# Recurrence of the gated linear attention: forward logarithm and scan moved ahead of the backward gates, sigmoid's table loaded by a one-element activation

## The reference, cut to what matters

```
u = h @ w_in                          # 2048 x 10240
q, a_f, a_b, i, z = split(u, 5)
log_f = logaddexp(log(lb), log1p(-lb) + log_sigmoid(a))   # = log(lb + (1 - lb) * sigmoid(a))
key   = (1 - lb) * sigmoid(-a)
# forward and backward, per head: b = cumsum(log_f); scores = q k exp(b_t - b_s), t >= s; out = scores @ v
o = rms_norm(o_fwd + o_bwd, o_norm)
return (o * silu(z)) @ w_out
```

## Time and profile before

| | |
|---|---|
| Median of 3 runs | 1899.51 us (1898.82 to 1900.25) |
| Profiled execution, first to last instruction (span) | 1896.9 us |
| Runs' median less the span | 2.6 us |
| TensorE busy | 1891.0 us (100%) |
| VectorE, ScalarE, GpSimd busy | 1288.3, 1058.0, 624.8 us |
| Granted TensorE clock | full speed in all 40 slices |
| DMA | 352.64 MB, mean 186 GB/s |

### The profile page before, as it was taken

The page is one execution under the profiler, slowest core; times in us unless marked ns, Lnnn a source line. Parts: engine busy times, 40 slices in busy tenths (PEclk is TensorE's granted clock), DMA queues, the critical chain, the costliest instruction groups (busy, mean ns, idle before and its releaser), DMA issues.

```text
span 1896.9 us, 28820 instructions
## 1 busy us (share of the span) xinstructions
PE 1891.0 (100%) x10856; PEld 1558.4 (82%) x10856; DVE 1288.3 (68%) x1871; ACT 1058.0 (56%) x1402; POOL 624.8 (33%) x657
## 2 busy tenths in 40 slices
PE   9999999999999999999999999999999999999999
PEld 8888878888887888788888888888888888888887
DVE  5899967555888888887668876555555555544443
ACT  7444466456868787875465755444444444443432
POOL 1899852306051423302408643222222222210000
PEclk9999999999999999999999999999999999999999
DMA  9666656666555565555565555666666666666564
GB/s 326 193 190 186 178 170 196 189 194 183 168 175 166 151 187 166 169 158 187 189 189 147 155 177 176 201 193 195 188 192 196 194 192 193 194 193 195 192 196 157
DMA packets 183600, 352.64 MB, mean 186 GB/s; under 512 B 11840, under 2 KB 12352, under 8 KB 183488
## 3 DMA queue, kind: packets, MB, share of 16 engines
q1 hardware_dynamic: 183344, 351.12, 61.1%
q10 hardware_dynamic: 144, 0.01, 0.0%
HBM read 348.99 MB, written 2.10 MB: 185 GB/s over the span
## 4 chain that ended last, share of the span: by engine, by line
PE 88%; DVE 4%; POOL 4%; issue 2%; ACT 2%; DVEq 1%; POOLq 0%; ACTq 0%
PE acc L625 28%; PE acc L627 28%; PE acc L626 28%; POOL kb L503 2%; POOL kf L503 1%; DVE w_lo L1271 1%; PE T L576 1%; DVEq L1257 1%; PE acc L592 1%; PE T L740 1%; PE T L841 0%; ACT w_hi L887 0%; PE T L731 0%; DVE Xc L1459 0%; PE T L820 0%
## 5 line engine op out<-in xcount | busy, mean ns | idle before, releaser
L1271 DVE TENSOR_TENSOR w_lo<-raw,w_hi 128x1024 fp32r<-128x1024 f32 x564 | 695.2, 1235 | 516.5 <-ACT w_hi L887 507.3
L887 ACT ACTIVATE w_hi<-raw 128x1024 fp32r<-128x1024 f32 x655 | 687.5, 1057 | 609.8 <-PE acc L627 587.4
L625 PE MATMUL acc<-w_hi,h_hi 128*128 128x512 f32 x1872 | 735.5, 393 | 1.1 <-DVE w_lo L1271 1.0
L627 PE MATMUL acc<-w_hi,h_lo 128*128 128x512 f32 x1872 | 728.8, 389 | 0.0
L626 PE MATMUL acc<-w_lo,h_hi 128*128 128x512 f32 x1872 | 728.7, 389 | 0.0
L625 PEld LDWEIGHTS acc<-w_hi,h_hi 128*128 128x128 f32 x1872 | 351.4, 188 | 80.4 <-issue 4.5
L627 PEld LDWEIGHTS acc<-w_hi,h_lo 128*128 128x128 f32 x1872 | 351.4, 188 | 73.7
L626 PEld LDWEIGHTS acc<-w_lo,h_hi 128*128 128x128 f32 x1872 | 351.5, 188 | 71.1
L565 POOL COPY fT<-fq 32x256 f32<-32x256 f32 x176 | 110.9, 630 | 387.4 <-DVE fq L1753 380.5
L474 POOL TENSOR_TENSOR w_lo<-raw,w_hi 128x1024 fp32r<-128x1024 f32 x80 | 190.5, 2411 | 68.0 <-ACT w_hi L887 67.8
L1362 DVE SCALAR_TENSOR_TENSOR T<-vpad,feat,T 128x256 f32<-128x256 f32 x464 | 182.5, 482 | 0.0
(11 more groups left out here) (256 smaller groups left out, 1564.8 us busy)
## 6 DMA issues: line engine op xcount, KB each, us to landing
raw<-in_hgrn_w_in_dram SPq DMA_DIRECT2D x160, 512.0 KB, 3.7
raw<-in_conv_w_in_dram SPq DMA_DIRECT2D x96, 512.0 KB, 4.2
raw<-in_ffn_w_gate_dram SPq DMA_DIRECT2D x88, 512.0 KB, 4.4
raw<-in_ffn_w_up_dram SPq DMA_DIRECT2D x88, 512.0 KB, 4.3
raw<-in_ffn_w_down_dram SPq DMA_DIRECT2D x88, 512.0 KB, 4.2
raw<-in_attn_w_qkv_dram SPq DMA_DIRECT2D x40, 512.0 KB, 3.7
raw<-in_conv_w_out_dram SPq DMA_DIRECT2D x32, 512.0 KB, 4.4
raw<-in_hgrn_w_out_dram SPq DMA_DIRECT2D x32, 512.0 KB, 4.5
```

The costliest lines, as they stand in the source:

```text
L625: nc.tensor.matmul(o, hi[:, kt, a], w_hi[:, slot, kk, :], start=c == 0 and kk == 0, stop=False)
L627: last = nc.tensor.matmul(o, lo[:, kt, a], w_hi[:, slot, kk, :], start=False, stop=c == p.chunks - 1 and kk == CK - 1)
L887: A(w_hi[:, slot, :, :], raw[:, slot, :, :], ACT.Copy).then_inc(hi_ready, 1)
L1271: TT(w_lo[:, slot, :, :], raw[:, slot, :, :], rounded(w_hi[:, slot, :, :]), ALU.subtract).then_inc(split_ready, 1)
```

## The change: what it does

- `ln_f(j, 0)` moves from hook 6 to hook 3 (behind `raw_out`), and waits for `gates(j, 0)` alone; `ln_f(j, 1)` stays at hook 7. The order of `g_act` is now gates 0, ln 0, gates 1, ln 1.
- `scan_f` moves on VectorE from hook 8 to hook 5, `bounds_of` from hook 2 to hook 1 (ahead of `o_scale`).
- At hook 6, ahead of the waits of `gates(j, 1)`, a sigmoid of one element per partition is written to a tile `primed` that nothing reads.

```
-        sb(ctx, "align_turned", [P, 24])
+        primed = sb(ctx, "primed", [P, 1])
+        sb(ctx, "align_turned", [P, 23])
...
             def gates(j, d):
 
+                if d == 1:
+                    A(primed[:, :], eps[:, 0:1], ACT.Sigmoid)
+                    act.wait_ge(g_q, 3 * j + 3)
                 act.wait_ge(g_M, 3 * j + 1 + d)
-                if d == 1:
-                    act.wait_ge(g_q, 3 * j + 3)
...
             def ln_f(j, d):
 
                 act.wait_ge(g_lb, j + 1)
-                act.wait_ge(g_act, 6 * j + 2)
+                act.wait_ge(g_act, 6 * j + 2 * d + 1)
...
-                at = Hooks().put(1, lambda: gates(j, 0)).put(6, lambda: gates(j, 1))
+                at = Hooks().put(1, lambda: gates(j, 0)).put(3, lambda: ln_f(j, 0)).put(6, lambda: gates(j, 1)).put(7, lambda: ln_f(j, 1))
                 for d in range(2):
-                    at.put(6 + d, lambda d=d: ln_f(j, d)).put(8 + d, lambda d=d: ln_k(j, d))
+                    at.put(8 + d, lambda d=d: ln_k(j, d))
...
             def diagonal(j):
 
                 dve.wait_ge(g_lb, j + 1)
-                dve.wait_ge(g_act, 6 * j + 2)
+                dve.wait_ge(g_act, 6 * j + 3)
...
             def scan_f(j):
 
-                dve.wait_ge(g_act, 6 * j + 3)
+                dve.wait_ge(g_act, 6 * j + 2)
...
-                at = Hooks().put(2, lambda: bounds_of(j)).put(6, lambda: diagonal(j)).put(8, lambda: scan_f(j)).put(9, lambda: scan_b(j))
+                at = Hooks().put(1, lambda: bounds_of(j)).put(5, lambda: scan_f(j)).put(6, lambda: diagonal(j)).put(9, lambda: scan_b(j))
```

## The result

The changed kernel takes **1910.35 us** (median of 5 runs, 1910.31 to 1910.64) beside 1899.39 us for the kernel before, measured with it: a ratio of 1.0062, 95% interval 1.0052 to 1.0073. It is 11 us slower, where 3.5 us faster was forecast and the range ended at 1898.3.

The account below looks back on a forecast made before the run. TensorE was taken to bound the kernel, its 4.8 us of waits for weight loads being all to win; less 10 x 0.13 for ten gaps, 3.5 us, so 1899.5 to 1896.0 us, range 1895.0 to 1898.3.

Parts of the forecast that it names:

- The change, part by part: Walk through each moved step in group 1 of the recurrence, giving what each costs or hides; all gaps close.
- Added work: Two more table loads and one primer per group: 11 us of ScalarE's time, none of it where TensorE waits.
- the one on the other side: Rival 4: kb finishes late under scan and w_lo, delaying gates(1) before chunk 7; 2.5 us slower, 1902.0; chance 0.05.
- signs of being right: No w_lo wait above 0.1 us, levels 19.0 to 19.1 us apart, w_hi 8 about 6.3 us after gates(1), 5 loads a group.
- the ceiling of 3.5 us: TensorE's waits for weight loads in the recurrence, 4.8 us in ten gaps, worth 3.5 us in all.
- ln_f(0) to hook 3: Table load and four logarithms, 3.3 us, moved behind vtok on ScalarE: cost nothing, with 4 us of cover.
- scan_f to hook 5: Scan of 2.43 us on VectorE from 565.5 to 567.9; w_lo of chunk 6 slips, diagonal isn't later: cost nothing.
- the narrow margin of 0.35 us at chunk 7: In group 1, w_lo of chunk 7 was to end at 574.75, 0.35 before TensorE wants it at 575.10.
- the 0.13 by which each counts for less: In chunks 9 to 13, two gaps reading 1.43 us cost 1.17, so each gap counts 0.13 less than it reads.
- Rival 3: The scan holds up GpSimd's kb copies, making gates(1) 0.7 later, with gaps before chunk 7: about 1897.2 us; chance 0.15.
- The primer: Table load of 1.29 and one-element activation of 0.20 at hook 6, hidden in ScalarE's idle in group 1, not everywhere.
- The table: A table load on ScalarE lasts 1.28 us with no drain around it, against the skill page's 2.66 us in all.

Follow-up runs that it names:

- r2: The kernel before with only the two layout lines, an unused one-element tile and the pad at 23, no instruction differing: 1912.62 us beside 1898.28.
- r12: r1's file (tiles at their old addresses) with scan_f back at hook 8: 1895.47 us beside 1898.57 for the kernel before.
- r1: The changed kernel with the pad at 16 elements instead of 23, so every later tile has its old SBUF address: 1896.31 us beside 1898.28 before.
- r14: r1's file with scan_f at hook 8 and no primer: 1896.33 us beside 1898.57 for the kernel before.

## Why the prediction was wrong

- **The step that failed: "The change, part by part".** It went through every moved step and had no term for the first lines of the diff, the new tile and the pad of 23. I took the pad's 24 - 1 elements as the old layout. It isn't: the two shift all later tiles by 32 bytes, which measured **+14.3 us** alone (r2). "Added work" said that none of it lay where TensorE waits; the cost lay in TensorE's own pace, 227 ns from matmul to matmul becoming 233 in 184 chunks, none of them in the recurrence. No rival held it either; the one on the other side was late `kb`, which didn't happen. Two of the prediction's signs of being right, levels 19.06 us apart and five loads a group, came true in a kernel that was 14 us over the forecast: signs taken from the stretch that was edited can't show a loss elsewhere.
- **What bounds the kernel in the recurrence, and the ceiling of 3.5 us:** right. In r12 the waits on `w_lo` are nearly gone, and 3.1 us are won (3.2 by its trace, between the first and the last level). That the pace of a busy TensorE would stay as it was went unsaid, and that was the error.
- **ln_f(0) to hook 3, costing nothing:** right by the traces. Its table load starts at 559.37 in r1 and the chain behind `gates(1)` is early enough for chunks 8, 10 and 13: no gap there in any group.
- **scan_f to hook 5, "cost nothing":** wrong by a little. Its duration was taken from hook 8 (2.43); beside GpSimd's copies it is 3.09, and the narrow margin of 0.35 us at chunk 7 became gaps of 0.47, 0.17 and 0.35 in r1. With the 0.2 and 0.3 us before chunk 2 in groups 1 and 2, less the 0.13 by which each counts for less, they are 0.8 us: 3.5 - 0.8 = 2.7, and 2.7 is what r1's trace wins between the first and the last level. The 0.7 from there to the 2.0 between the medians is no more than the runs of either kernel spread. I hadn't looked at chunk 2.
- **Rival 3** had the right pair and the wrong victim. In group 1 of r1 the eight copies of `kb` take 8.9 us (before: 10.18) and are done at 566.8, just when ScalarE comes free, so the gates aren't late. The scan meets mostly the copies of `qT` and gets slower itself.
- **The primer:** right that it costs TensorE next to nothing (r12 has one gap more than r14, 0.17 us in group 2). For a load behind the wait the prediction had 1.3 us, of which 0.5 would be lost in a group; where that happens, in one group of r14, 1.18 us are.
- **The table:** a load costs 1.28 us with nothing around it in the trace after, too, though there are two more a group: ScalarE's busy time grew by 12.3 us, and r12, which has all of these loads, keeps 3.1 of the 3.5 us. The 2.66 us of the Trainium skill's page "ScalarE: Activation LUTs" ("What ACT_TABLE_LOAD costs") aren't seen.

## What to carry to other kernels

Read a diff's allocations as steps: a tile of 4 bytes moved 184 chunks' stationary tiles, and cost seven times what the schedule won. Tiles named as pads are a sign that somebody measured; compute the start of each tile before and after. When TensorE is busy longer with the same count of matmuls at the same clock, count matmuls in equal windows of each phase, and look for the operand that the slow phases share.

## What was not expected of the hardware

- The pace of a 128x128 by 128x512 fp32r matmul depends on the distance of its two SBUF operands: 443 in 100 us where it is a multiple of 256 bytes, 428 to 432 where it is off by 32 to 128, and as much so while no other engine or DMA is active.
- A scan of 128x256 takes 0.81 us (median of 16, r1 and the changed kernel) at hook 5, beside GpSimd's copies, and 0.66 at hook 8 (r12). A copy of 32x256 takes 0.70 us beside it (r1), where it takes 0.40 while VectorE is idle, so both sides lose. The pair wasn't tried by itself, outside this kernel. The Trainium skill's page "SBUF — State Buffer", section "Who interferes with whom", names the contention of a VectorE instruction with two SBUF inputs and a GpSimd one that reads; these rows agree with it.
